# The second norm of a hybrid decoder layer split between ScalarE and VectorE, with more transpose buffers and an earlier reload of X

## What is computed

```python
merged = gate_a * (pa @ w_pool_out) + gate_b * (sg @ w_gmlp_out)
x = x + merged @ w_out
h2 = rmsnorm(x, g_ffn)          # x * rsqrt(mean(x*x) + EPS) * g_ffn, row by row
x = x + (silu(h2 @ w_gate) * (h2 @ w_up)) @ w_down
y = rmsnorm(x, g_final)
```

## Time and profile before

| | |
|---|---|
| median of 3 runs | 787.89 us (787.49 to 789.29) |
| the profiled execution | 787.72 us; span of the slowest core 786.2 us |
| TensorE (PE) busy | 760.3 us, 97% of the span |
| VectorE (DVE) busy | 546.9 us, 70% |
| ScalarE (ACT) busy | 337.4 us, 43% |
| GpSimd (POOL) busy | 124.9 us, 16% |
| spans of the 8 cores | 782.1 to 786.2 us |

### The profile page before, as it was taken

How to read it: one execution, slowest core, us unless ns; L and a number is a source line. 1 busy time by engine, 2 the same in 40 slices (tenths; PEclk the granted TensorE clock), 3 DMA queues, 4 the chain that set the end, 5 groups by cost and what they waited for, 6 DMA issues and landing times.

```text
span 786.2 us, 14620 instructions; the slowest of 8 cores (782.1 to 786.2 us)
## 1 busy us (share of the span) xinstructions
PE 760.3 (97%) x4852; PEld 446.8 (57%) x4852; DVE 546.9 (70%) x1039; ACT 337.4 (43%) x730; POOL 124.9 (16%) x201
## 2 busy tenths in 40 slices
PE   8989999999999999949999999999999999999996
PEld 4544545666666654426666446666644566666443
DVE  3699988777777667687767546766643376766776
ACT  4595555544544423234553005555400155554333
POOL 4153421000000012452100011000100200100111
PEclk9999999999999999968999999999999999999998
DMA  9973448221212067848432007322200173220244
GB/s 187 253 232 67 69 72 122 37 43 30 41 28 42 14 97 167 169 91 141 83 50 42 1 1 113 49 41 42 45 11 0 22 114 55 42 41 1 111 161 160
DMA packets 48891, 60.66 MB, mean 77 GB/s; under 512 B 28209, under 2 KB 28721, under 8 KB 48802
## 3 DMA queue, kind: packets, MB, share of 16 engines
q0 software_dynamic: 15840, 28.84, 24.1%
q1 hardware_dynamic: 32542, 30.58, 14.8%
q10 hardware_dynamic: 436, 0.31, 0.1%
HBM read 73.64 MB, written 9.01 MB: 105 GB/s over the span
## 4 chain that ended last, share of the span: by engine, by line
PE 89%; DVE 4%; issue 3%; ACT 2%; DMA 1%; POOL 1%; DVEq 0%; POOLq 0%; ACTq 0%; SPq 0%
PE ps L466 85%; DVE hb L502 1%; ACT junk L487 1%; PE ps L1152 1%; DVE X L497 1%; DMA hT<-hb 1%; PE ps L956 1%; POOL rs L614 1%; DVE actr L497 1%; PE ps L749 1%; ACT Fb L487 0%; PE ps L643 0%; PE ps L972 0%; DVE mrg L502 0%; DVE Fb L497 0%
## 5 line engine op out<-in xcount | busy, mean ns | idle before, releaser
L466 PE MATMUL ps<-hT,ring 128*128 128x344 f16 (+4 forms) x1428 | 232.6, 312 | 2.4 <-ACT hT L487 1.0
L487 ACT ACTIVATE Fb<-ps 128x344 f32<-128x344 f32 (+3 forms) x278 | 129.2, 468 | 221.9 <-PE ps L466 192.7
L466 PE MATMUL ps<-ring,mrg 128*128 128x512 f16 (+1 forms) x976 | 212.0, 377 | 1.1 <-DVE X L497 1.1
L497 DVE TENSOR_TENSOR Fb<-Fb,ps 128x344 f32<-128x344 f32 x304 | 150.9, 510 | 52.0 <-ACT Fb L487 32.4
L466 PEld LDWEIGHTS ps<-hT,ring 128*128 128x128 f16 x1428 | 134.0, 99 | 80.9 <-issue 4.7
L497 DVE TENSOR_TENSOR X<-X,ps 128x512 f32<-128x512 f32 (+3 forms) x173 | 109.4, 640 | 80.7 <-PE ps L466 77.9
L466 PEld LDWEIGHTS ps<-ring,mrg 128*128 128x128 f16 x976 | 95.0, 98 | 112.4 <-issue 2.2
L521 POOL DMA_DIRECT2D ring<-wpk x107 | 56.9, 544 | 416.2 <-PE ps L466 403.8
L487 ACT ACTIVATE Fb<-Fb 128x344 f32<-128x344 f32 x174 | 84.8, 487 | 84.6 <-DVE Fb L497 82.6
L466 PE MATMUL ps<-actr,ring 128*128 128x344 f16 x600 | 109.6, 310 | 0.0
L487 ACT ACTIVATE junk<-X 128x1025 f16<-128x1025 f32 (+4 forms) x53 | 54.5, 1029 | 88.7 <-DVE X L497 86.1
(11 more groups left out here) (126 smaller groups left out, 583.8 us busy)
## 6 DMA issues: line engine op xcount, KB each, us to landing
ring<-wpk POOLq DMA_DIRECT2D x107, 256.0 KB, 5.0
X<-xp SPq DMA_DIRECT2D x25, 512.0 KB, 6.5
yp<-actr SPq DMA_DIRECT2D x15, 512.0 KB, 2.7
actr<-cst SPq DMA_DIRECT2D x2, 512.0 KB, 4.7
mrg<-cst SPq DMA_DIRECT2D x2, 256.0 KB, 9.8
mrg<-cst SPq DMA_DIRECT2D x1, 512.0 KB, 9.4
hb<-wpk POOLq DMA_DIRECT2D x2, 256.0 KB, 3.8
nps<-st SPq DMA_DIRECT2D x1, 448.0 KB, 10.2
```

Source lines behind the costliest of these rows:

```text
L466: ins = e.matmul(out=ap, lhsT=l, rhs=rr, start=(start and i == 0), stop=(stop and i == len(pairs) - 1), skip_group_check=skip)
L487: return e.activation(out=P.r(out), in_=P.r(in_), func=func, scale=scale, **kw)
L497: return P.add(eng, lambda e: e.tensor_tensor(out=P.r(out), in0=P.r(a), in1=P.r(b), op=op), reads=[a, b], writes=[out], dur=vdur(n, per), ...
```

## The change

1. `norm` gets a second form (`two=True`), used for the second norm: ScalarE multiplies the row by its factor into the fp16 buffer, and VectorE multiplies that buffer in place by norm weights in fp16.
2. The norm weights are loaded to another place and turned into fp16 by one VectorE copy before the first norm of the stage. Weights of the second and of the final norm no longer share a place.
3. Six transpose buffers in place of three; the new ones are rows 1 to 3 of `Fb`.
4. The nine tiles of X are reloaded with a priority that puts them ahead of the stage, without a wait for transposes.
5. `half_sums` is no longer split: all its sums are on VectorE.
6. The first two weight pairs of the feed-forward network are loaded after the transpose of tile 10, not after the last weight of the output projection.

```diff
-        gffn = actr[:, 6, 0:2048].bitcast(F32)
+        gffn = actr[:, 7, 0:2048].bitcast(F32)
+        gfin = actr[:, 6, 0:2048].bitcast(F32)
...
-        gfin = gffn
...
-        def norm(t, grep, prio, xbar=True):
+        def norm(t, grep, prio, xbar=True, two=False):
...
-            ho = vstt(hbs[hi][:R, :], X[:R, XR(t), 0:D], r, grep[:R, :], ALU.mult, ALU.mult, prio, D)
+            if two:
+                act(hbs[hi][:R, :], X[:R, XR(t), 0:D], AF.Copy, prio, scale=r)
+                ho = vtt(hbs[hi][:R, :], hbs[hi][:R, :], grep[:R, :], ALU.mult, prio, D, per=0.52)
+            else:
+                ho = vstt(hbs[hi][:R, :], X[:R, XR(t), 0:D], r, grep[:R, :], ALU.mult, ALU.mult, prio, D)
...
-        hbs.append(wsbs[:, :])
+        hbs += [wsbs[:, :]] + [Fb[:, i, 0:512].bitcast(F16) for i in range(1, 4)]
+        gffn16 = actr[:, 6, 0:1024]
+        vcopy(gffn16, gffn, 1950.0, D)
+        for t in sorted(range(NT), key=XR)[7:]:
+            xload(t, prio=1990.0)
...
-            h_last = norm(t, gffn, pr + 1.0)
-            if t < NT and XR(t) + 7 < 16:
-                xload([t_ for t_ in range(NT) if XR(t_) == XR(t) + 7][0], after=[P.ops[h_last.i + 1]])
+            h_last = norm(t, gffn16, pr + 1.0, two=True)
+            h3[t] = h_last
...
-                half_sums(hsum, j, pr + 25.0, split=j < 2, mg=600.0)
+                half_sums(hsum, j, pr + 25.0, mg=600.0)
...
-                aft = () if gi else [P.ops[h_last.i + 1]] if fl >= 2 else [wo_last]
+                aft = () if gi else [P.ops[h_last.i + 1]] if fl >= 2 else [P.ops[h3[10].i + 1]]
```

More of the change, by code:

```diff
@@ L548, in build_nc, with xload @@
         x_dma = {}
-        def xload(t, after=()):
+        def xload(t, after=(), prio=None):
+            prio = -10.0 + 0.1 * t if prio is None else prio
             if t < NT:
-                o_ = dma('sp', X[:, XR(t), 0:D], xp[t * 128:(t + 1) * 128, :], 'x%d' % t, 524288, -10.0 + 0.1 * t, after)
+                o_ = dma('sp', X[:, XR(t), 0:D], xp[t * 128:(t + 1) * 128, :], 'x%d' % t, 524288, prio, after)
             else:
-                o_ = dma('sp', X[:NSMP, XR(t), 0:D], xs[:, :], 'x%d' % t, 65536, -10.0 + 0.1 * t, after)
+                o_ = dma('sp', X[:NSMP, XR(t), 0:D], xs[:, :], 'x%d' % t, 65536, prio, after)
             x_dma[t] = o_
@@ L981, in build_nc @@
         act(samW, pv, AF.Copy, 2000.6, n=128)
-        hbs.append(wsbs[:, :])
+        hbs += [wsbs[:, :]] + [Fb[:, i, 0:512].bitcast(F16) for i in range(1, 4)]
[3 more added lines that the diff above has]
+            xload(t, prio=1990.0)
         order3 = []
+        h3 = {}
         for t in range(8):
```

## The result

The changed kernel takes **781.75 us** (781.44 to 782.25 in four executions) against 787.69 for the kernel before beside it; the ratio is 0.9924, with a 95% interval of 0.9905 to 0.9943. It is faster by 5.9 us.

The account below looks back on a forecast made before the run. The prediction saw TensorE full except for a hole at the output projection's end, where VectorE was late. Cutting its 15.6 us to 4.1 gains 11.5, so 787.9 - 11.5 gives 776.5 us, range 773.5 to 783.5.

Parts of the forecast that it names:

- The hole: End of the output projection, before the feed-forward network: TensorE idles 11.6 us and then runs at half clock, costing 15.6 us.
- The sum: TensorE's loss at the projection's end falls from 15.6 us to 4.1 at full clock, a gain of 11.5 us.
- the lowered clock: After TensorE's long wait at the projection's end, matmuls run at half clock; priced at 4.0 us.
- zero for PE: Norm weights, eighth in the reload burst, land near 288 us; VectorE's copy costs 1 us, TensorE loses nothing.
- The cover: Eight PSUM banks give TensorE 14 us of work while VectorE handles the norm weights; if it fails, +3 us.
- ScalarE's round: Second norm, per tile: square, power, scaling and hand-overs take 3.2 to 3.4 us, under TensorE's 3.5.
- VectorE is relieved of 10 us: Second norm in two steps: VectorE swaps 17 norms of 1.28 us for fp16 multiplies of 0.69.
- net relief: Half-sums off GpSimd: VectorE gains 3.5 us of work but loses about 6.8 us of stretching.
- (a): Rival, chance 0.15: TensorE's clock falls all the same, from four close waits of 0.7 to 1.4 us; 780.5 us.
- (b): Rival, chance 0.10: transposes stay slow among the weight loads, 4.7 us instead of 3.2; 780 to 785, say 782.
- (c): Rival, chance 0.05: no difference, the last tile's chain stays as long because ScalarE is late by 11 us; 787.5.
- (d): Rival, chance 0.08: slower, ScalarE's round per tile exceeds 3.5 us and sets the pace; 791 us.

Follow-up runs that it names:

- early_weights: The changed kernel with the first two feed-forward weight pairs issued at the start of the output projection, as before the change; 786.3 us, ratio 0.9971.
- one_step: The changed kernel with the second norm in one VectorE instruction again, with fp32 weights and no scaling on ScalarE; 782.4 us, ratio 0.9924.
- three_bufs: The changed kernel with three transpose buffers, as before the change, in place of six; 780.8 us, ratio 0.9903.
- pool_sums: The changed kernel with half of the third and fourth half-sums of the first two slices on GpSimd again; 787.5 us, ratio 0.9991.
- before_unsplit: The kernel before with one part of the change alone, all half-sums on VectorE and none on GpSimd; 782.3 us, ratio 0.9926.

## Why the prediction was right in sign and short in size

**The hole was priced on one core, and it was the worst.** This is the term of the sum that was mis-sized, and it cost most. The sum took 15.6 us of loss from the slowest core. TensorE's waits for ScalarE's copies on core 0 of the same execution (waits, 284 to 362 us, before, to be set beside the 10.5 of the earlier trace rows):

```profile
PE ps L466 <- ACT Fb L487: 8.7, 2, 8.0
```

On core 7 the rest fell from 512.2 to 500.6, by 11.6 us, the 11.5 of the sum almost to the tenth; that it is this close is in part luck, since core 7 is the worst core before and one of the best after. The mean rest fell from 510.0 to 502.0, by 8.0. TensorE's waits from 284 to 368 us went from 10.0 to 4.9 us on the mean of the cores, and from 11.6 to 3.8 on core 7; the other 2.9 of the 8.0 lie outside these waits, the lowered clock among it, which the sum put at 4.0 (TensorE's granted clock is at half for a time in this stage on all eight cores before, and on one after).

A core's whole span gains less again. In the profiled executions the changed kernel's cores reach the split point some 1 us later on the mean (275.3, before 274.2), and the profiled execution of the kernel before was itself above the common one: over 23 other executions, on another chip, the cores' mean span is 783.3, over the four of the changed kernel 777.15, so a core gains 6.1 on average. The slowest core is now one that lost 4 to 5 us before the stage: core 3's 780.7 is 278.9 to the split point plus 501.8, where core 7 before had 274.0 plus 512.2.

**The burst was not free.** I put the norm weights, eighth in the burst, at "zero for PE" with 288 us as their landing. On core 7 they do land at 288.2, and VectorE waits 2.1 us for them. Over the eight cores of the changed kernel:

| core | 2 | 4 | 3 | 7 | 6 | 1 | 5 | 0 |
|---|---|---|---|---|---|---|---|---|
| VectorE's wait for the norm weights, us | 0.8 | 1.2 | 2.0 | 2.1 | 2.7 | 2.8 | 3.3 | 3.8 |
| rest, us | 500.4 | 500.4 | 501.8 | 500.6 | 502.8 | 501.9 | 503.3 | 504.6 |

On core 0 (VectorE, then the DMA issue, then TensorE, after):

```profile
293.12 0.69 DVE L513 CAST actr<-actr 128x1024 f16<-128x1024 f32 x1 [3.81 <-DMA actr<-cst]
```

```profile
actr<-cst SPq DMA_DIRECT2D x1, 512.0 KB, 11.8
```

```profile
341.62 0.74 PE L466 MATMUL ps<-actr 128*128 128x344 f16 x4 [2.14 <-ACT Fb L487]
```

The cover held, since PSUM took TensorE through the wait; the lag did not go away. ScalarE's round for a tile takes 3.0 us beside TensorE's 3.5, so it makes up half a microsecond a tile, and GpSimd's four weight issues of 0.55 us each take some of that back in the middle of the stage. The mean over cores is 1.6 us above the best two. early_weights moved the landing later, and the rest went to 506.0 to 509.6 on six of eight cores; moving it earlier, ahead of the reloads, was not tried, so that the weights alone account for the spread is likely, not shown (one core of early_weights waited 4.4 and had a rest of 501.8). The Trainium skill, DMA: Bandwidth & Descriptors, Queues, rings and completion order, says that each ring's descriptors are taken in order; the 3.7 us without loads ahead and the 11.8 behind eight of them agree.

**The parts' credit was wrong, their durations right.** Scaling 1.15 us (1.16 taken), multiply 0.69 (0.69), ScalarE's round 3.03 (3.2 to 3.4), last add 2.8 us behind TensorE (2.0), last transpose landed 11.6 behind it (11.0), waits 3.84 (4.1). Yet "VectorE is relieved of 10 us" is worth nothing (one_step), the three new buffers bring nothing (three_bufs), and "net relief" of 3.3 us for the sums carries the whole gain (pool_sums, before_unsplit). The prediction lists the reliefs of VectorE side by side and tests none against the others; once the sums are unsplit VectorE has room, and the second relief buys only idle time. It also names the stretching as the sums' cost and not the order that the planner makes with them, which before_unsplit shows at work.

**The rivals.** (a) The clock fell on one core of eight. On core 0 TensorE idled 2.1 us up to 341.62, and the level behind it was 0.50 (busy time by stretch, core 0, after):

```profile
340.00:342.00 2.00, 0.38 (x3) 0.31 (x4) 1.63 (x4) 1.48 (x2) 0.00 (x0) 1.00 0.69 129
...
344.00:346.00 2.00, 2.00 (x9) 0.95 (x7) 0.00 (x0) 1.99 (x4) 0.46 (x1) 0.50 0.27 47
```

The four waits that I thought might do it, close together, left core 7 at 1.00. (b) Held in part: beside the weight loads the two transposes issued between 314 and 318 us on core 7 took 5.5 us at the median, but VectorE did not wait for them. (c) did not come, and (d) neither in the changed kernel: ScalarE's round is under TensorE's. ScalarE can be late without a longer round: in early_weights it still takes 3.0 us a tile and ends behind because VectorE started late.

## What to carry to other kernels

Price a hole on every core, and on more than one execution, before it is set against a time that is the slowest core's: take the mean loss as the gain, and ask which core will be the slowest next. Reliefs of one engine need not add: here, after the first that gave it room, the rest bought idle time; so of a bundle, try each part alone, and begin with the work on GpSimd that runs beside VectorE. Where a planner orders the engines, compare the orders too: in before_unsplit one word moved an add ahead of a norm and a half-sum. In a burst of loads, look at where the one stands that is needed first (putting it first was not tried here); a wait that PSUM hides from TensorE can come back at the end of the stage when the engine that waited has little slack per tile.

## What the runs showed of the hardware

- Beside GpSimd's sums VectorE's fp16 instructions with two SBUF inputs took two to four times as long: 1.97 us for a multiply of 1024 columns (0.69 alone), 1.85 for a sum of 1376 (0.87), 1.62 for a sum of 512 (0.42). They end 0.3 to 0.7 us after the GpSimd sum in which they started (pool_sums, 55 of 55), so they seem to wait for it; adds out of PSUM stayed at 0.68.
- The time that a load took to land followed what stood ahead of it and beside it: 512 KB landed after 3.7 us alone, after 8.1 to 11.8 behind eight reloads and after 17.3 with four weight loads beside them.
- The clock does not answer to the length of one wait alone: it fell to 0.50 behind a wait of 2.1 us (core 0, after) and stayed at 1.00 through one of 3.8 us on core 7 of three_bufs, which ends in the second of these rows (busy time by stretch):

```profile
340.00:342.00 2.00, 0.00 (x0) 0.00 (x0) 2.00 (x3) 0.62 (x3) 1.14 (x1) 1.00 0.10 23
342.00:344.00 2.00, 0.53 (x4) 0.41 (x5) 1.63 (x4) 1.33 (x2) 0.00 (x0) 1.00 0.78 112
344.00:346.00 2.00, 2.00 (x16) 1.33 (x15) 1.53 (x4) 1.51 (x3) 0.24 (x1) 1.00 0.54 100
```
